# mLSTM and attention block on one core: the two halves of the output projection added up in one bank, w_out kept on chip, tiles reversed and turned first

## The reference

```
h = rms_norm(x, pre_norm_g)
aq, ak, av, az, mq, mk, mv, mo, mz, mi, mf = split_columns(h @ w_in)   # 9 x 512 columns, 2 x 4
ya = moba_attention(rope(aq), rope(ak), av)      # 8 heads of 64, causal
ya = rms_norm(ya, attn_out_g) * silu(az)
hm = mlstm_chunkwise(mq_c, mk_c, mv, mi, mf)     # 4 heads of 128, after a convolution and silu
ym = sigmoid(mo) * head_norm(hm) * mlstm_out_g * silu(mz)
y = concatenate([ya, ym]) @ w_out
x = x + rms_norm(y, post_norm_g)
```

## Time and profile before

| what | value |
|---|---|
| median of 3 runs | 334.77 us (334.74 to 335.21) |
| the profiled execution's own time | 335.24 us |
| its span, first to last instruction | 333.5 us |
| PE busy | 317.8 us, 95% of the span |
| DVE, ACT, POOL busy | 227.5, 172.2, 99.9 us |
| granted clock of PE, mean | 0.992 of full speed |
| chain that ended last, by engine | PE 84%, DVE 9%, issue 4%, ACT 2% |
| first step (scores of units 0 and 1) | at 209 us |

### The profile page before, as it was taken

The page is one execution under the profiler, slowest core; times in us unless marked ns, Lnnn a source line. Parts: engine busy times, 40 slices in busy tenths (PEclk is TensorE's granted clock), DMA queues, the critical chain, the costliest instruction groups (busy, mean ns, idle before and its releaser), DMA issues.

```text
span 333.5 us, 5022 instructions
## 1 busy us (share of the span) xinstructions
PE 317.8 (95%) x1614; PEld 260.9 (78%) x1614; DVE 227.5 (68%) x530; ACT 172.2 (52%) x341; POOL 99.9 (30%) x121
## 2 busy tenths in 40 slices
PE   8999999999999999899999999999999998998790
PEld 5887788888888888688888888788888887887580
DVE  2544999678996589876995487575766743435785
ACT  3448653696373524845346522655548647354330
POOL 8001003207240240002400054880025724154451
PEclk9999999999999999999999999999999999999996
DMA  7931544842736552246425232200001401602044
GB/s 225 286 96 32 166 129 107 164 140 82 127 85 157 147 87 64 63 126 132 76 63 159 70 89 66 90 37 2 0 2 63 172 19 43 211 23 105 0 156 160
DMA packets 26873, 33.51 MB, mean 100 GB/s; under 512 B 3752, under 2 KB 15056, under 8 KB 26848
## 3 DMA queue, kind: packets, MB, share of 16 engines
q1 hardware_dynamic: 25712, 30.51, 30.6%
q0 software_dynamic: 1120, 2.68, 6.2%
q10 hardware_dynamic: 16, 0.00, 0.0%
HBM read 31.06 MB, written 2.13 MB: 100 GB/s over the span
## 4 chain that ended last, share of the span: by engine, by line
PE 84%; DVE 9%; issue 4%; ACT 2%; DVEq 0%; POOLq 0%; POOL 0%; ACTq 0%
PE bank L1355 21%; PE bank L1357 21%; PE bank L1356 21%; PE bank L1402 3%; PE bank L1646 3%; PE bank L1696 3%; PE bank L1667 2%; PE bank L1490 1%; PE bank L1383 1%; PE bank L1370 1%; DVE farena L1043 1%; DVE xT_lo L1213 1%; PE bank L1657 1%; ACT xT_hi L801 1%; DVE w_lo L922 1%
## 5 line engine op out<-in xcount | busy, mean ns | idle before, releaser
L1355 PE MATMUL bank<-w_hi,xT_hi 128*128 128x512 f32 x272 | 110.7, 407 | 0.0
L1357 PE MATMUL bank<-w_hi,xT_lo 128*128 128x512 f32 x272 | 106.7, 392 | 0.0
L1356 PE MATMUL bank<-w_lo,xT_hi 128*128 128x512 f32 x272 | 106.1, 390 | 0.0
L708 ACT ACTIVATE w_hi<-w_raw 128x512 fp32r<-128x512 f32 x88 | 53.2, 626 | 59.2 <-PE bank L1357 58.8
L1357 PEld LDWEIGHTS bank<-w_hi,xT_lo 128*128 128x128 f32 x272 | 51.0, 188 | 11.4
L1355 PEld LDWEIGHTS bank<-w_hi,xT_hi 128*128 128x128 f32 x272 | 51.2, 188 | 9.1 <-issue 0.4
L1356 PEld LDWEIGHTS bank<-w_lo,xT_hi 128*128 128x128 f32 x272 | 51.3, 189 | 8.8
L922 DVE TENSOR_TENSOR w_lo<-w_raw,w_hi 128x512 fp32r<-128x512 f32 x64 | 45.1, 719 | 5.0 <-ACT w_hi L708 4.5
L591 POOL TENSOR_TENSOR w_lo<-w_raw,w_hi 128x512 fp32r<-128x512 f32 x24 | 31.2, 1320 | 48.4 <-ACT w_hi L708 48.4
L862 ACT ACTIVATE rarena<-bank 128x512 fp32r<-128x512 f32 (+3 forms) x32 | 13.8, 435 | 26.0 <-PE bank L1696 26.0
L1256 DVE CUSTOM_DVE_ANT_0 farena<-bank,causal 128x512 f32<-128x512 f32 (+3 forms) x32 | 15.4, 483 | 17.1 <-PE bank L1646 17.1
(11 more groups left out here) (195 smaller groups left out, 522.8 us busy)
## 6 DMA issues: line engine op xcount, KB each, us to landing
w_raw<-in_w_in SPq DMA_DIRECT2D x72, 256.0 KB, 2.9
w_raw<-in_w_out SPq DMA_DIRECT2D x16, 256.0 KB, 2.7
farena<-in_x SPq DMA_DIRECT2D x4, 256.0 KB, 4.7
farena<-in_x SPq DMA_DIRECT2D x2, 512.0 KB, 7.5
farena<-g_rows POOLq DMA_DIRECT2D x4, 256.0 KB, 3.9
silu_az<-in_x SPq DMA_DIRECT2D x2, 512.0 KB, 3.7
w_raw<-in_x SPq DMA_DIRECT2D x2, 512.0 KB, 3.3
out_y<-silu_az SPq DMA_DIRECT2D x4, 256.0 KB, 2.0
```

Source lines behind the costliest of these rows:

```text
L708: a.activation(w_hi[:, n % RING, :], w_raw[:, n % RAW, :], ACT.Copy).then_inc(w_hi_done, 1)
L1355: pe.matmul(o, hi, m_hi, start=start, stop=False)
L1356: pe.matmul(o, hi, m_lo, start=False, stop=False)
L1357: return pe.matmul(o, lo, m_hi, start=False, stop=stop)
```

## The change

Names in the rows below: `rarena` holds mLSTM operands, keys, values and transposed probabilities; `farena` float32 scratch; `gy` the gates and ym; `stage` keys, queries, later the post gain; `wg` the weights of the two small gates.

- **One bank.** `out_part` replaces `om_part` and `oa`: the eight parts (four of ym, four of ya) of one tile's half of the columns accumulate in one bank. `om_evac` and `y_sum` are gone. `ya_gate` (DVE) multiplies ya by its norm's factor before the turn, for all four tiles; a product on POOL (first two tiles) or DVE (last two) without that factor is gone. ACT squares straight from the bank, and `y_gain` on DVE multiplies the bank by the post gain; POOL does no gain any more.
- **w_out on chip.** All 16 slots stay: `out_home` puts them in the ring and in areas that have become free (pairs in `rarena`, `wg`). ACT's and POOL's cuts of them stand at steps 5 to 8 (four) and 13 to 20 (twelve) instead of 15 to 18 (eight), 23 and 27 (four each).
- **Tiles reversed.** z, ym and the turns go from tile 3 to tile 0, like the attention.
- **Spread.** z is done by step 15 (3 parts a step in steps 2 to 5, then 2), the output takes 2 parts a step in steps 16 to 34.
- **Turns first.** All turns are at odd steps and are the step's first work on PE, ACT and, behind mask and value sum, on DVE.
- **The end.** The last half of the last tile is made as two quarters of 256 columns in banks 5 and 7, with their own squares, gains and stores, one from ACT's queue.
- **Keys.** `kt_high` of the first two tiles stands one and two slots earlier on ACT, `kt_low` likewise on DVE.
- **Residuals** go into `gy`, loaded early.

```diff
-for _r in (4, 0):
-    SLOTS += [("out", "cols", _r + k, c * AW) for c in range(2) for k in range(4)]
-S_MV, S_AZ, S_AK, S_AV, S_AQ, S_MZ, S_MO, S_OM, S_OA = 0, 12, 24, 36, 48, 56, 64, 72, 80
+for _c in range(2):
+    SLOTS += [("out", "cols", _r + k, _c * AW) for _r in (4, 0) for k in range(4)]
+S_MV, S_AZ, S_AK, S_AV, S_AQ, S_MZ, S_MO, S_OUT = 0, 12, 24, 36, 48, 56, 64, 72
...
+PARTS = {2: 3, 3: 3, 4: 3, 5: 3}
+PART_AT = [s for s in range(2, 16) for _ in range(PARTS.get(s, 2))]
+OUT_CUTS = {0: 5, 1: 6, 2: 7, 3: 8, 12: 17, 13: 17, 14: 19, 15: 20}
...
-TURNS = sorted([(PART_AT[NK * _t + NK - 1] + 4, "ym", _t) for _t in range(NT)] + [(23, "ya", 0), (25, "ya", 1),
-                                                                                  (31, "ya", 2), (36, "ya", 3)])
+for _n in sorted(OUT_CUTS):
+    _event(OUT_CUTS[_n], "cut", S_OUT + _n)
+
+TURNS = sorted([((PART_AT[NK * _n + NK - 1] + 4) // 2 * 2 + 1, "ym", _n) for _n in range(NT)] + [
+    (17, "ya", 0), (25, "ya", 1), (33, "ya", 2), (37, "ya", 3)])
...
-OA_ORDER = ((0, 0, 27), (1, 0, 28), (0, 1, 30), (1, 1, 33), (2, 0, 35), (2, 1, 36), (3, 0, 37), (3, 1, 38))
-OA_OF = {(_i, _c): _n for _n, (_i, _c, _at) in enumerate(OA_ORDER)}
-for _i, _c, _at in OA_ORDER:
-    for _k in range(4):
-        _event(_at, "oa", _i, 4 * _c + _k)
-    _event(_at + int(_at < 35), "y", _i, _c)
-    _event(_at + 1, "y_sq", _i, _c)
-for _i, (_mean, _end) in enumerate(((33, 34), (35, 36), (37, 37), (39, 39))):
+
+
+def _twos(s):
+    return [s + k // 2 for k in range(NK)]
+
+
+OUT_ORDER = ((0, 0, _twos(16), 20), (0, 1, _twos(20), 24), (1, 0, _twos(24), 28), (1, 1, _twos(28), 32),
+             (2, 0, [32, 32, 33, 33, 34, 34, 35, 35], 36), (2, 1, [35] * 4 + [36] * 4, 37),
+             (3, 0, [37] * 4 + [38] * 4, 39), (3, 1, [37] * 4 + [39] * 4, 40))
...
+    if (_i, _c) == (NT - 1, 1):
+        for _q in range(2):
+            for _k in range(NK):
+                _event(_at[_k], "part_q", _q, _k)
+            _event(_sum_at + _q, "y_q", _q)
+            _event(_sum_at + _q, "y_q_sq", _q)
+        continue
+    for _k in range(NK):
+        _event(_at[_k], "part", _i, _c, _k)
+    _event(_sum_at, "y", _i, _c)
+    _event(_sum_at, "y_sq", _i, _c)
+for _i, (_mean, _end) in enumerate(((25, 26), (33, 34), (38, 38), (41, 41))):
     _event(_mean, "y_fin", _i)
-    _event(_end, "y_end", _i)
+    for _c in range(2):
+        _event(_end, "y_end", _i, _c)
...
-    _event(_s + 1 + 4 * _late, "ya_sq", _i)
-    _event(_s + 2 + 4 * _late, "ya_ms", _i)
+    _event(_s + 3 * _late, "ya_sq", _i)
+    _event(_s + 1 + 3 * _late, "ya_ms", _i)
+    _event(_s + 1 + 4 * _late, "ya_gate", _i)
...
+        def out_home(n):
+
+            pairs = r_part(R_OUT, 4, SEQ)
+            wide = wg[:].rearrange("p k c -> p (k c)")
+            if n < 2:
+                return blocks(pairs[:, 2 * n]), blocks(pairs[:, 2 * n + 1])
+            if n == 2:
+                return blocks(wide[:, 0:AW]), blocks(wide[:, AW:])
+            if n in (3, 13):
+                i = n // 13
+                return blocks(qT[:, 2 * i]), blocks(qT[:, 2 * i + 1])
+            if n in (12, 14):
+                at = (3 - n // 14) * AH
+                return v_hl[:, at:at + 4], v_hl[:, at + 4:at + 8]
+            if n == 15:
+                return kT_hi[:, :, (NT - 1) * P:], kT_lo[:, :, (NT - 1) * P:]
+            return blocks(w_hi[:, n - 4]), blocks(w_lo[:, n - 4])
...
-            sp.wait_ge(turn_ps, TURN_OF["ya", 1] + 1)
+            sp.wait_ge(ym_gated, NT)
             load_residual(0)
-            for i in (1, 2):
-                low_done(sp, NSLOT - RAW + 2 * i - 2)
-                low_done(sp, NSLOT - RAW + 2 * i - 1)
-                load_residual(i)
+            load_residual(1)
+            sp.wait_ge(turn_ps, TURN_OF["ym", NT - 1] + 1)
+            load_residual(2)
+            load_residual(3)
             store(sp, 0)
             store(sp, 1)
-            sp.wait_ge(out_done[0], 32)
-            load_residual(3)
             store(sp, 2)
-            store(sp, 3)
+            sp.wait_ge(out_ready, 2 * NT - 1)
+            sp.dma_start(out[0, 0:P, 0:AW], xr[NT - 1][:, 0:AW]).then_inc(out_done[NT - 1], 16)
+            sp.wait_ge(out_ready, 2 * NT + 1)
+            sp.dma_start(out[0, 0:P, quarter[1]], xr[NT - 1][:, quarter[1]]).then_inc(out_done[NT - 1], 16)
...
-                g.wait_ge(ya_done, i + 1)
-                g.wait_ge(az_gained, t + 1)
-                g.tensor_tensor(silu_az[:, t, :], ya[:, i % 2, :], silu_az[:, t, :], ALU.mult).then_inc(ya_gated, 1)
-
-            def y_gain(i, c):
-
-                n = OA_OF[i, c]
-                g.wait_ge(post_in, 16)
-                g.wait_ge(ssy_done, n + 1)
-                g.tensor_tensor(yb[:, i % 2, c * AW:(c + 1) * AW], yb[:, i % 2, c * AW:(c + 1) * AW],
-                                post[:, c * AW:(c + 1) * AW], ALU.mult).then_inc(y_gained, 1)
...
+                if KT_AT + 1 <= b < KT_AT + 3:
+                    kt_high(a, b - KT_AT - 1)
...
-        def om_evac(a, n):
-
-            c, t = n // NT, n % NT
-            projected(a, "om", n)
-            a.wait_ge(turn_ps, TURN_OF["ym", t] + 1)
-            a.wait_ge(ym_gated, t + 1)
-            a.activation(y_mlstm[:, c, t, :], shared("om", n)[:], ACT.Copy).then_inc(om_done, 1)
...
+                if b == KT_AT + 1:
+                    kt_low(0)
...
+                if b == KT_AT + 2:
+                    kt_low(1)
...
+            def ya_gate(i):
+
+                t = NT - 1 - i
+                v.wait_ge(ya_done, i + 1)
                 v.wait_ge(ra_done, i + 1)
+                v.wait_ge(az_gained, NT)
+                v.scalar_tensor_tensor(out=silu_az[:, t, :], in0=ya[:, i % 2, :], scalar=ra[:, i:i + 1],
+                                       in1=silu_az[:, t, :], op0=ALU.mult, op1=ALU.mult).then_inc(ya_gated, 1)
+
+            def y_gain(i, c):
+                n, cols = OUT_OF[i, c], slice(c * AW, (c + 1) * AW)
+                v.wait_ge(ssy_done, n + 1)
+                v.wait_ge(post_in, 16)
                 if i >= 2:
                     v.wait_ge(out_ready, 2 * (i - 1))
-                v.scalar_tensor_tensor(out=yb[:, i % 2, cols], in0=shared("oa", n)[:], scalar=ra[:, i:i + 1],
-                                       in1=y_mlstm[:, c, NT - 1 - i, :], op0=ALU.mult, op1=ALU.add).then_inc(y_done, 1)
+                v.tensor_tensor(yb[:, i % 2, cols], shared("y", n)[:], post[:, cols], ALU.mult).then_inc(y_done, 1)
...
+            def out_part(i, c, k):
+
+                n, slot = OUT_OF[i, c], S_OUT + NK * c + k
+                turned(i, k)
+                low_done(pe, slot)
+                if k == 0:
+                    shared_free("y", n)
+                mm = product(blocks(shared("y", n)[:]), *x_part(k, NT - 1 - i), *out_home(slot - S_OUT), k == 0,
+                             k == NK - 1)
+                if k == NK - 1:
                     mm.then_inc(oa_ps, 1)
+
+            def out_quarter(q, k):
+
+                slot = S_OUT + NK + k
+                turned(NT - 1, k)
+                low_done(pe, slot)
+                if k == 0 and q == 0:
+                    pe.wait_ge(pt_lo, NU)
+                elif k == 0:
+                    pe.wait_ge(masked, NU)
+                hi, lo = out_home(slot - S_OUT)
+                mm = product(blocks(bank[(5, 7)[q]][:])[:, 0:2], *x_part(k, 0), hi[:, 2 * q:2 * q + 2],
+                             lo[:, 2 * q:2 * q + 2], k == 0, k == NK - 1)
+                if k == NK - 1:
+                    mm.then_inc(oaq_ps, 1)
...
+                for kind, what in events:
+                    if kind == "turn":
+                        turn(*what)
                 u = s - LAG_T
```

More of the change, by code:

```diff
@@ L112 @@
 EVENTS = {}
-PRIORITY = ("mz", "mz_late", "z", "om_out", "cut", "slot", "z_part", "om", "oa", "q_T", "q_out", "ya_half", "y", "ya", "y_sq", "ya_sq",
-            "ya_ms", "y_fin", "y_end", "turn")
+PRIORITY = ("mz", "mz_late", "z", "slot", "z_part", "part", "part_q", "q_T", "q_out", "ya_half", "ya", "ya_sq", "ya_ms",
+            "ya_gate", "y_sq", "y", "y_q_sq", "y_q", "y_fin", "y_end", "cut", "turn")
 def _event(step, kind, *what):
@@ L652, in _ @@
                         rsqrt(ra[:, i:i + 1], msa[:, i:i + 1]).then_inc(ra_done, 1)
-                    elif kind == "y_sq" and i < NT - 1:
-                        y_gain(*what)
                     elif kind == "y_fin":
@@ L1342, in _ @@
                         ya_scale(*what)
+                    elif kind == "ya_gate":
+                        ya_gate(*what)
                     elif kind == "y":
-                        y_sum(*what)
-                    elif kind == "y_fin":
+                        y_gain(*what)
+                    elif kind == "y_q":
+                        y_quarter(*what)
+                    elif kind == "y_fin" and what[0] < NT - 1:
                         y_mean(*what)
@@ L1702, in _ @@
                 for kind, what in events:
-                    if kind == "turn":
```

(2 more changed lines are left out.)

238 lines of the change are left out of this document (130 added, 108 removed).

## The result

The changed kernel takes 326.23 us (326.02 to 326.27, 4 runs) against 334.75 us before (334.70 to 335.21, 4 runs): ratio 0.9741, 95% interval 0.9724 to 0.9758, 8.5 us faster.

What follows compares the result with a forecast made beforehand. PE bounds the kernel, busy 317.8 of 333.5 us, so gains come from its waits and the tail. -1.2 - 2.4 - 4.0 + 0.2 + 0.4 - 2.4 = -9.4 us: span 324.1, median 325.4 us, range 323.8 to 328.7.

Steps and rivals of the forecast that it cites:

- Keys, -1.2 us: Key turn near 137 us: moving the key cuts earlier removes PE's wait for `kt_low(0)`, 1.0 + 0.16; bounds 0 to 1.2.
- Turns first, -2.4 us: Four waits of scores for a turned tile, 2.5 us with overlap, go almost wholly; bounds 0 to 2.5.
- The doubtful turn: Step 17's turn: two ACT cuts just ahead wait for loads, so one of eight turns is short of room; 0.1 allowed.
- Steps 28 to 36, -4.0 us: Three PE waits (step 30's scores, last values, last turn), 1.3 + 1.3 + 0.9 + 3 x 0.16, go; bounds 1.1 to 4.0.
- new waits, +0.4: Denser DVE steps and the twelve w_out cuts: 0.2 us each; bounds 0 to +2.7 and 0 to +1.5.
- Quarters, +0.2 us: Last half: 48 matmuls of 256 columns replace 24 of 512, loads hidden; upper bound +3.5 if every load stood alone.
- The tail, -2.4 us: Behind PE's last matmul: 5.4 us against 7.8; bounds 1.2 (DVE no longer late, nothing else) to 2.8.
- half-width matmuls show their loads: Rival, last half's 256-column matmuls: weight loads not hidden, +3.3 over the 0.2 counted, 328.7 us; chance 0.04.
- The waits move to DVE: Rival, short steps: mask or turn_lo late at bursts, waits of steps 30 and 34 return, 328.3 us; chance 0.24.
- The ring holds ACT: Rival, w_out cuts: one waiting for its load keeps back ACT's exponentials, 335.6 us at 8 us landing; slower, chance 0.04.
- No change: Rival, all waits: causes only look like order, 0.5 us gained in the tail beside new waits, 334.6 us; chance 0.02.
- two signs of being altogether wrong: PE's 256-column matmuls starting more than 0.15 us apart, or DVE's `y_gain` waiting for the post gain.

Runs made afterwards that it cites:

- changed, keys back: Changed kernel with the two moves of `kt_high` and `kt_low` undone, back to their old slots: 327.26 us.
- before, turns first: Kernel before, with the turned tile put first within each step on PE, ACT and DVE, steps of the turns unchanged: 332.64 us, ratio 0.9930.

## Why the prediction was right

325.4 (323.8 to 328.7) was predicted, 326.23 measured. The span of the profiled execution, 324.1, is the sum's to the tenth, but this is partly luck. The last matmul was put at 318.7 and the tail at 5.4; they are 318.13 and 5.85, and the two errors nearly cancel. The three columns of the table show the rest: the change brings 1.05 (keys), 5.94 (steps) and 1.98 us (tail), 9.0 in all, and the other 0.4 of the 9.4 is that the profiled execution of the kernel before came late to its first scores.

- **Keys, -1.2 us.** Measured 1.03 (taken back) and 1.1 (alone). Right in mechanism; 0.1 to 0.2 too much, because the 1.0 us that the sum starts from is the wait of that one execution, and it is 0.87 in "changed, keys back" and in "before, turns first".
- **Turns first, -2.4 us.** 2.0 in the steps and 2.25 in the median, alone. In the changed kernel it is 1.8, where no wait is like the longest before, 0.93 us at 283 us behind ACT's two cuts of the earlier trace rows. The doubtful turn, at step 17, fitted although ACT stood at a cut for its load just before. ACT and DVE there, then PE (ACT's `turn_high` is L822, DVE's low half L1272):

```profile
260.39 0.63 ACT L882 ACTIVATE w_hi<-w_raw 128x512 fp32r<-128x512 f32 x1 [0.62 <-DMA w_raw<-in_w_out]
260.93 0.58 ACT L822 ACTIVATE xT_hi<-bank 128x512 fp32r<-128x512 f32 x1
```

```profile
261.54 0.69 DVE L1272 TENSOR_TENSOR xT_lo<-bank,xT_hi 128x512 fp32r<-128x512 f32 x1
```

```profile
259.68 0.60 PE L1691 MATMUL bank<-ident,silu_az 128*128 128x128 f32 x4
...
262.37 0.62 PE L1740 MATMUL bank<-rarena 64*128 64x256 f32 x6
```

  The low half ends at 262.2, the scores start at 262.37: some 0.15 us of room, in place of the 0.3 to 0.9 counted.
- **Steps 28 to 36, -4.0 us, and new waits, +0.4.** The steps shrank by 5.94 us in all. Less 2.0 for the order and with 0.16 for the quarters taken off again, 4.1 us remain for both terms together, where the sum had 3.6. 1.9 of them are shown to be GpSimd's product beside DVE's. The rest, 2.2, fits the wait of the last values (1.3 + 0.16), what is left of step 30 (0.4 + 0.16) and the turn that still waited (0.2 + 0.16), 2.4 by the rows, but it is argued, not isolated. **New waits** is the term that was mis-sized here: PE has no wait at all behind the start-up. DVE's share in 280 to 300 rose to 12.68 of 20 us and still stayed off PE's path. The last turn, at 306.61, stands 7.1 us behind the last values, with no idle time before it (the estimate had 6.9 us for PE's parts there against 4.5 of DVE and ACT); DVE's gate before it starts at 303.45:

```profile
299.49 0.34 PE L1773 MATMUL bank<-rarena 128*128 128x128 f32 x2
...
306.61 0.60 PE L1691 MATMUL bank<-ident,silu_az 128*128 128x128 f32 x4
```

- **Quarters, +0.2 us.** 0.16 measured. The loads of weights for 256 columns are hidden; PEld's timeline in the last half us, where PE starts a matmul each 0.12 us:

```profile
317.78 0.19 PEld L1443 LDWEIGHTS bank<-rarena,xT_hi 128*128 128x128 f32 x1
317.90 0.19 PEld L1444 LDWEIGHTS bank<-rarena,xT_hi 128*128 128x128 f32 x1
```

  The nearest row was the right one, and the upper bound of 3.5 us was far off.
- **The tail, -2.4 us.** -1.98: 5.85 us in place of 5.4. With the last half whole it is 6.58, so 1.25 of the gain comes without quarters and 0.73 with them. That the 1.25 meets the lower bound of 1.2 ("DVE no longer late, nothing else") is chance, for two things changed in it. The square starts 0.19 us behind PE's end and not 2.03 (327.70 less 325.67), which is 1.84: DVE is no longer late, and its sum of 0.75 us stands no longer before the square. Against that, 1.80 us pass from the square to the power (318.22 to 320.02) where 1.23 did (327.70 to 328.93), since the gain on DVE now comes before the mean. The tail is 0.4 us longer than the sum had it. Along the chain: PE's end to the square 0.19, square 0.47, handoff 0.11, DVE's sum to GpSimd's power 0.24, power 0.54, output from 319.84 to 321.38, last store issued at 321.41, end 2.69 behind it:

```profile
318.44 0.38 ACT L950 ACTIVATE gains<-bank 128x256 f32<-128x256 f32 x1 [0.93 <-PE bank L1445]
...
319.02 0.16 DVE L1380 SCALAR_TENSOR_TENSOR msy<-ssq,msy 128x1 f32<-128x1 f32 x1 [0.74 <-ACT gains L950]
...
319.26 0.54 POOL L592 TENSOR_TENSOR ry<-msy,mhalf 128x1 f32<-128x1 f32 x1 [9.17 <-DVE msy L1380]
319.84 1.54 DVE L1396 SCALAR_TENSOR_TENSOR gy<-farena,ry,gy 128x512 f32<-128x512 f32 x3 [0.26 <-POOL ry L592]
...
321.41 0.33 SPq L546 DMA_DIRECT2D out_y<-gy  x1
```

  The sum had 0.1 us for handoffs; the two beside PE's end and behind the square alone are 0.3. Store and end were put at 2.45.
- **From the span to the median.** The kernel before was profiled in an execution 0.5 us above its median, and the table shows where: at the first scores it is 0.55 us later than two kernels with the same instructions up to there. The changed kernel's profiled execution is at its median (326.21 against 326.23). So 0.4 to 0.5 us of the fall in the span is scatter, which the prediction subtracted once more to reach the median; the change itself took about 9.0 us off the span, not 9.4. The other 0.35 us are outside the span. Together they are the 0.8 us between 325.4 and 326.23. The step of the prediction with the largest error is "the median shown is 0.5 lower, so I predict 325.4": it takes both the scatter and the time outside the span to be carried over.

Of the rivals, "half-width matmuls show their loads" falls to the 0.12 us starts. "The waits move to DVE" falls to the waits table. "The ring holds ACT" has its mechanism but not its size: ACT does idle at cuts for a load, 0.28 to 0.62 us each around 257 to 263.5 us, but in its own slack, and PE does not wait. "No change" falls to every row. Of the two signs of being altogether wrong neither came: matmuls of 256 columns start 0.12 us apart, and DVE's waits behind 205 us hold none for a load, so the post gain was in time.

## What to carry to other kernels

- When PE is the bound, list its waits and follow each to the late instruction; waits whose causes are separate add up (1.1, 2.0 and 1.9 us here, alone and together). Add the overlap that each forfeits, and count handoffs in a tail one by one, and what stands between them on each engine.
- A long elementwise product is a candidate for what ran beside it: removing six GpSimd products that nobody waited for won 2.0 us, as much as reordering eight turned tiles.
- Compare kernels by stages between marks that both have. Stages repeat to 0.1 us where a single profiled execution carries 0.5 us of start-up scatter, and a prediction should start from the profiled execution's stage times and the median's total, not mix the two.
